# Two four-tile channel sums of the spatial unit, moved from TensorE's accumulation to GpSimd additions

## The reference, cut to what matters

```python
def layer_norm(x, g, b):
    mu = jnp.mean(xf, axis=-1, keepdims=True)
    xc = xf - mu
    var = jnp.mean(xc * xc, axis=-1, keepdims=True)
    return xc * lax.rsqrt(var + EPS) * g + b

y_cm, v_rows = sgu_branch(jax.nn.gelu(u), jax.nn.gelu(v), ...)   # v: 512 channels, normalised over the channels
```

## Time and profile before

| | us |
|---|---|
| median of 3 runs | 1589.9 (1588.88 to 1589.93) |
| profiled execution | 1589.27 |
| span of its trace | 1587.4 |
| PE busy | 1561.0 (98%) |
| DVE busy | 1068.7 (67%) |
| ACT busy | 884.6 (56%) |
| POOL busy | 521.1 (33%) |

### The profile page before, as it was taken

The page is one execution under the profiler, slowest core; times in us unless marked ns, Lnnn a source line. Parts: engine busy times, 40 slices in busy tenths (PEclk is TensorE's granted clock), DMA queues, the critical chain, the costliest instruction groups (busy, mean ns, idle before and its releaser), DMA issues.

```text
span 1587.4 us, 33215 instructions
## 1 busy us (share of the span) xinstructions
PE 1561.0 (98%) x10860; PEld 1516.9 (96%) x10860; DVE 1068.7 (67%) x1626; ACT 884.6 (56%) x1612; POOL 521.1 (33%) x659
## 2 busy tenths in 40 slices
PE   7999999999999999999999999999999999999999
PEld 7987999999999999999999789999999999999999
DVE  6787777777664766664376877777775748666633
ACT  5786676767534444443357866666764345444432
POOL 3732377776700000000058213767667001000000
PEclk9999999999999999999999999999999999999999
DMA  7331455553544444444454224655535444444443
GB/s 274 120 108 52 139 183 167 163 161 109 186 134 155 151 147 146 150 155 146 146 188 136 76 73 137 196 152 166 163 111 174 145 154 151 147 146 146 151 152 112
DMA packets 114690, 232.90 MB, mean 147 GB/s; under 512 B 12881, under 2 KB 78706, under 8 KB 114450
## 3 DMA queue, kind: packets, MB, share of 16 engines
q1 hardware_dynamic: 112178, 223.13, 45.3%
q0 software_dynamic: 2400, 8.36, 1.6%
HBM read 228.98 MB, written 2.46 MB: 146 GB/s over the span
## 4 chain that ended last, share of the span: by engine, by line
PE 90%; DVE 4%; ACT 2%; DVEq 1%; issue 1%; ACTq 1%; DMA 0%; POOL 0%; SPq 0%; POOLq 0%
PE PS L803 53%; PE PS L1048 26%; PE PS L1081 2%; PE PS L1082 2%; DVE w_lo L1742 1%; PE PS L1043 1%; ACT w_hi L1297 1%; DVEq L1736 1%; PE PS L830 1%; PE PS L859 1%; ACTq L1301 0%; ACT r_hi L1297 0%; PE PS L937 0%; ACTq L1485 0%; DMA x<-in_xT 0%
## 5 line engine op out<-in xcount | busy, mean ns | idle before, releaser
L1742 DVE TENSOR_TENSOR w_lo<-raw,w_hi 128x1024 fp32r<-128x1024 f32 x258 | 325.0, 1261 | 222.9 <-ACT w_hi L1297 220.0
L1297 ACT ACTIVATE w_hi<-raw 128x1024 fp32r<-128x1024 f32 x258 | 272.3, 1057 | 347.3 <-PE PS L803 333.1
L803 PE MATMUL PS<-h_hi,w_hi 128*128 128x320 f32 x1360 | 426.4, 314 | 11.1 <-DVE h_lo L1769 10.3
L803 PE MATMUL PS<-h_hi,w_lo 128*128 128x320 f32 x1360 | 421.3, 310 | 0.0
L803 PE MATMUL PS<-h_lo,w_hi 128*128 128x320 f32 x1360 | 421.3, 310 | 0.0
L803 PEld LDWEIGHTS PS<-h_hi,w_hi 128*128 128x128 f32 x1360 | 256.3, 188 | 14.2 <-issue 9.5
L803 PEld LDWEIGHTS PS<-h_lo,w_hi 128*128 128x128 f32 x1360 | 256.4, 189 | 0.9
L803 PEld LDWEIGHTS PS<-h_hi,w_lo 128*128 128x128 f32 x1360 | 256.2, 188 | 0.0
L1048 PE MATMUL PS<-comb_hi,lt_hi 128*128 128x288 f32 x1024 | 239.9, 315 | 0.0
L1297 ACT ACTIVATE ksqp<-PS 128x512 f32<-128x512 f32 x256 | 153.2, 598 | 152.4 <-PE PS L1048 150.3
L2097 DVE TENSOR_REDUCE kss<-ksqp 128x8 f32<-128x512 f32 x256 | 174.2, 682 | 85.3 <-ACT ksqp L1297 84.2
(11 more groups left out here) (317 smaller groups left out, 2662.0 us busy)
## 6 DMA issues: line engine op xcount, KB each, us to landing
raw<-in_stream SPq DMA_DIRECT2D x258, 512.0 KB, 3.5
tpage<-in_tcache SPq DMA_DIRECT2D x256, 192.0 KB, 2.4
rrow<-in_rcache SPq DMA_DIRECT2D x256, 128.0 KB, 2.6
x<-in_xT SPq DMA_DIRECT2D x2, 640.0 KB, 6.9
sbias<-in_sbias POOLq DMA_DIRECT2D x2, 640.0 KB, 6.2
out_yT<-x SPq DMA_DIRECT2D x4, 320.0 KB, 2.2
const<-in_consts SPq DMA_DIRECT2D x1, 1088.0 KB
wgate<-in_wgate POOLq DMA_DIRECT2D x2, 512.0 KB, 4.5
```

Of the source, the lines that this page charges most:

```text
L803: done = mm(out, w[:, slot, c], a, start=first and n == 0 and m == 0, stop=last and n == len(pairs) - 1 and m == 2)
L1297: return nc.scalar.activation(out, in_, func, **kw)
L1742: V.tensor_tensor(w_lo[:, s, :], raw[:, s, :], f(w_hi[:, s, :]), ALU.subtract).then_inc(lo_done.sem, 1)
```

## The change

GpSimd gets four additions per layer, TensorE loses six of eight products.

- Behind its cast of the key weights, GpSimd now waits for `gelu`, adds tiles 0 and 1 of `va` to tiles 2 and 3 in one instruction (128x640) into `tmp8[:, 2:4]`, drains, adds these two (128x320), and signals `v_added`. The low part of the key weights, the DMAs and the zeroing of `qz` stand behind that.
- Behind the zeroing of `qz`, GpSimd waits for the squares (`varsq`) and for the scaled queries (`qn_ready`), adds the four tiles of squares likewise into `qn[:, 0]`, and signals `v_added` again. The copies of the rotary queries stand behind that.
- The mean product becomes one product, after a wait for the first signal. The variance product becomes one product, after a wait for the second, and moves behind the key norm sums and the absorbed queries, to the end of `project`.

```diff
+    v_added = Signal("sgu_tiles_added", 2)
             nc.gpsimd.tensor_copy(comb_hi[:, :, :, 32:288], wk_raw[:])
+            pool.wait_ge(gelu.sem, gelu.at(l, 1))
+            pool.sem_inc(waits_passed, 1)
+            nc.gpsimd.tensor_tensor(tmp8[:, 2:4, :], va[:, 0:2, :], va[:, 2:4, :], ALU.add)
             pool.drain()
+            nc.gpsimd.tensor_tensor(tmp8[:, 2, :], tmp8[:, 2, :], tmp8[:, 3, :], ALU.add).then_inc(v_added.sem, 1)
             nc.gpsimd.tensor_tensor(comb_lo[:, :, :, 32:288], wk_raw[:], f(comb_hi[:, :, :, 32:288]), ALU.subtract).then_inc(wk_ready.sem, 1)
...
             nc.gpsimd.memset(qz[:], 0.0).then_inc(q_zeroed.sem, 1)
+            pool.wait_ge(varsq.sem, varsq.at(l, 1))
+            pool.sem_inc(waits_passed, 1)
+            pool.wait_ge(qn_ready.sem, qn_ready.at(l, 1))
+            pool.sem_inc(waits_passed, 1)
+            nc.gpsimd.tensor_tensor(qn[:, 0:2, :], ge[:, 0:2, :], ge[:, 2:4, :], ALU.add)
+            pool.drain()
+            nc.gpsimd.tensor_tensor(qn[:, 0, :], qn[:, 0, :], qn[:, 1, :], ALU.add).then_inc(v_added.sem, 1)
             pool.wait_ge(qpe_ready.sem, qpe_ready.at(l, 1))
...
             pe.wait_ge(bank_free[1].sem, banks.take(l, 1))
-            pe.wait_ge(gelu.sem, gelu.at(l, 1))
-            grouped(PS[:, 1, 0:T], ones[:], [va[:, j, :] for j in range(4)]).then_inc(mean_mm.sem, 1)
+            pe.wait_ge(v_added.sem, v_added.at(l, 1))
+            mm(PS[:, 1, 0:T], ones[:], tmp8[:, 2, :], start=True, stop=True).then_inc(mean_mm.sem, 1)
...
-            pe.wait_ge(bank_free[6].sem, banks.take(l, 6))
-            pe.wait_ge(varsq.sem, varsq.at(l, 1))
-            grouped(PS[:, 6, 0:T], ones[:], [ge[:, j, :] for j in range(4)]).then_inc(var_mm.sem, 1)
...
             last.then_inc(abs_mm.sem, 1)
+
+            pe.wait_ge(bank_free[6].sem, banks.take(l, 6))
+            pe.wait_ge(v_added.sem, v_added.at(l, 2))
+            mm(PS[:, 6, 0:T], ones[:], qn[:, 0, :], start=True, stop=True).then_inc(var_mm.sem, 1)
```

## The result

The changed kernel takes 1601.35 us in the median of four runs (1597.5, 1600.8, 1601.9, 1601.9) against 1589.91 for the kernel before on the same chip: ratio 1.0067, 95% interval 1.0052 to 1.0082. It is slower, as forecast, but by 11.4 us and not 6.4, and outside the range. The four runs are not alike. The profiled one is the fastest, with 1597.5 us, a span of 1595.7 and a mean granted clock of 0.998 of full speed; the other three have 0.993 to 0.996.

The account below looks back on a forecast made before the run. TensorE is 98% busy, but here the chain runs through VectorE and ScalarE, behind GpSimd's zeroing. Per layer 2.4 + 0.54 + 0.25 = 3.2 us, two layers 6.4: 1589.27 becomes 1595.7, plus 0.6 gives 1596.3 us; range 1592.5 to 1600.5.

Parts of the forecast that it names:

- Part 1: TensorE's mean and variance sums: one product instead of four, 1.63 us less each, 6.5 us of work in all.
- Part 2: GpSimd's first additions: zeroing of `qz` ends later, so VectorE's scaled queries start 2.4 us late (bounds 1.4 and 5.2).
- Part 3: VectorE and ScalarE pass the late zeroing on: key norm sums go from 97.81 to 100.2, TensorE idle.
- The wait foreseen ahead of the third key product: TensorE stops about 1 us there, for a bank freed by VectorE's scaling; inside the same delay.
- The start near 100.2: Sign of being right: in layer 0 the key norm sums (L919) start near 100.2; before 98.5 would be wrong.
- Part 4: Variance product behind the absorbed queries: 0.54 us a layer more on TensorE's path, 0 if another engine holds TensorE.
- Part 5: Second additions may hold VectorE's two small instructions: 0.25 us a layer taken, between 0 and 0.5.
- the slack named in the prediction: Behind VectorE's rotation: 0.23 us at L1922, 1.01 at ScalarE's first exponential, 0.54 from the variance product; 1.8 in all.
- I count no loss by the clock: TensorE's clock: no loss, as it was granted in full between 108 and 141 with 3.2 of 33 us idle.
- Much slower: GpSimd and VectorE block each other throughout: delay 5.2 instead of 2.4 us, 12.5 us in all, 1602.4; chance 12%.
- Faster: TensorE's work is the bound, so the four sums give back up to 6.5 us: 1583.4; chance 4%.
- no change: The delay is absorbed: low bound 3.9 us, partly taken up by idle time in the prompt's attention, about 1591.5; chance 12%.

Follow-up runs that it names:

- The mean alone: Changed kernel without the second additions, variance again by four products in the old place; 1593.65 us, ratio 1.0024 against the kernel before.
- the early zeroing: Changed kernel with the zeroing of `qz` and its waits moved ahead of GpSimd's wait for the key weights; 1590.51 us, ratio 1.0005.
- the filler: Changed kernel plus four products of ones and the cosine table, result unused, where the variance product stood; 1596.59 us, ratio 1.0039.
- the variance alone: Changed kernel without the first additions, mean again by four products; 1593.73 us, ratio 1.0029 against the kernel before.
- the variance product in its old place: Changed kernel with its single variance product ahead of the key norm sums, waiting for the second additions; 1600.6 us, ratio 1.0071.
- the moved product: Kernel before, no GpSimd additions, its four variance products moved behind the absorbed queries; 1597.85 us, ratio 1.0058.
- the early zeroing with the mean alone: Changed kernel with `qz` zeroed ahead of the additions, one mean product, four variance products in the old place; 1587.37 us, ratio 0.9987.
- the additions ahead of the cast: The kernel of 1587.37 us with GpSimd's additions moved ahead of its cast of the key weights; 1588.44 us, ratio 0.9999.

## Why the prediction was wrong

**Part 1 (1.63 us a sum less work for TensorE)** was right as work and, as said, not as time. The busy time fell by only 0.7 us, since 3.3 of 6.5 came back as slower key norm sums; what else kept it up was not singled out.

**Part 2 (the zeroing 2.4 us late)** was right in mechanism and nearly in size. The wide addition was held by VectorE's split as supposed (2.53 us; undisturbed the same form took 1.67), the narrow one took 0.88, the low part ran undisturbed in 2.41. From cast to end of zeroing 2.55 us were added; 2.9 was the prediction's figure. The scaled queries started right behind it.

**Part 3 (the delay reaches the key norm sums)**: right, 2.12 and 2.13 us. The mean alone paid it (3.9 us) and the early zeroing took it away (7.3 us with what hung on it). The wait foreseen ahead of the third key product is there, with 0.40 us and not about 1; one of 0.98 us ahead of the rotation was not foreseen; that ahead of the key norm sums, foreseen with over 2 us, is 3.18. Together TensorE idles 4.56 us in this stretch, 0.27 before. The start near 100.2 that was named came at 98.62 only because this execution began 1.3 us earlier.

**Part 4 (0.54 us a layer for the variance product on the path)**: right, 0.55 and 0.54.

**Part 5 (0.25 us a layer by blocking)**: the mechanism was there, the price was not. The small instruction of VectorE took 1.38 us instead of 0.22, held by the wide addition, and the second small one slipped through between the additions. The rotation started at 97.36, before the narrow addition at 97.44. From the recurrence's input (L1902) it is 1.1 us more than before; the slack named in the prediction covered it, and values to scores kept its 7.00 us, in the kernel with the early zeroing and full clock as well. The Trainium skill's rule of the shared ports (SBUF — State Buffer, "SBUF: two separate sides") agrees with the 1.38 us: the instruction ended at 97.11, GpSimd's at 97.04. But taken with the whole 2.3 us, as the prediction did for it, it charged 0.5 us a layer that did not come.

**The step that failed** is one sentence at the end of the sum: "I count no loss by the clock". It rested on the earlier trace rows, a stretch in which TensorE idled 3.2 of 33 us in many small pieces. The prediction itself had put over 2 us of idle time in one piece ahead of the key norm sums, behind another idle piece, with the four variance products gone that had lain there. It had called them cover for the path, and did not ask what they did for the clock. Measured, this costs 3.25 us in the profiled execution (1.69 + 1.56), and some 4 more in those near 1601 us. With the three parts as measured (2.1 + 0.55 + 0) the sum is 2 x 2.67 = 5.3 us, and from the profiled execution's 1589.27 it gives 1594.6 without the clock and 1597.9 with its 3.25, where the faster executions lie (1597.5 in the profile). The median of the first four runs was of the slower kind, that of the next six (1597.84) of the faster, and this one lies inside the range. Of all 12 runs of the changed kernel six took 1596.1 to 1597.9 us and six 1600.8 to 1603.1. So the clock's loss is in every traced execution, but that it carried the first median beyond 1600.5 is in part chance.

What supports the cause: the filler, which adds work and brings the key norm sums back to 2.42 us; the variance alone, slower by some 4 us in just the executions with a lower clock; and the kernel before with a moved product, which has no additions at all. All traces together, two layers each, say how the first products after the wait ran: at half clock at 10 of 10 places with 3.01 to 3.18 us of idle time ahead of them (the changed kernel four times, the variance product in its old place), at 3 of 6 with 2.43 or 2.44 us (the early zeroing, the variance alone, the moved product), at none of 12 with 0.27 to 1.02 us (the other six kernels). The Trainium skill (TensorE: Matmul & The Clock Gate, "Part 1: The HAM clock gate") says that the clock is full or half by how busy the engine has been of late, and that executions of one kernel can differ in it. The traces agree with both: 0.50 and 1.00 are the levels seen, and 2.43 us and 2.44 us of idle time had different ends.

**Rivals.** "Much slower" foresaw 1602.4 us, which three of the first four runs nearly had, but by VectorE and GpSimd blocking each other for 5.2 us a layer; the trace has 2.1, so its mechanism is refuted and the nearness an accident. "Faster" and "no change" fall with the wait of 2.58 us for the zeroing.

**What stays open.** Why one execution keeps the clock low for 4 us a layer and another for longer; and why half clock also comes at the end of the prompt's attention, where the change touches nothing. It was traced there in the mean alone, the filler, the moved product and the slower trace of the changed kernel, and in layer 1 of the variance alone (0.72 from 932 to 936 us) and of the additions ahead of the cast (0.53 from 924 to 926), while the faster traces of the changed kernel and the early zeroing with the mean alone have full clock. Two runs of the kernel before, 1591.4 us at clock 0.997 and 1592.7 at 0.998, suggest that it can happen without the change, but neither has a trace. A version that fills the waits of the prompt's attention was not tried.

## What to carry to other kernels

Work on an engine that waits anyway is free, but its removal need not be: ask whether it keeps TensorE's clock up, and price each longer idle piece with the next products at half speed. When work is handed to a helper engine, write down what stands behind it in that engine's list and who waits for it; here the fix was to put the one thing that others wait for (the zeroing) into the helper's idle time ahead of the new work. Take only the part of the saving that lies on the path: one mean product with the early zeroing gave 0.13%, the whole change took 0.67%.

## What the runs showed of the hardware

- The granted clock fell to a half after 2.43 to 3.18 us of idle time in the midst of a program that is 98% busy, and cost 1.6 us a layer in the changed kernel's first trace, 2.9 in its slower one; after 0.3 us (four products in the wait) and after 1.02 us (the filler) it did not.
- It need not fall after the same idle time: 2.43 us was followed by 0.50 in the traces of the variance alone and the moved product and by 1.00 in that of the early zeroing.
- A VectorE addition of 32 elements a partition took 1.38 us under a GpSimd addition of 640, 0.22 without. GpSimd's additions took 1.67 us for 640 elements and 0.86 to 0.88 for 320 when undisturbed; the prediction's line through its rows gave 1.57 and 0.875.
